# Two pairs of triangular inverses taken level by level together, and stores moved, in a two-layer decoder step

## Chip, cores and metric

The kernel runs on one NeuronCore of a Trainium2 chip (trn2). The metric is the device time of one execution in microseconds (us).

## What is computed

The program is one inference step of a two-layer hybrid decoder, for a prompt of 512 tokens and 8 samples of one token each (520 columns, model width 1024, all in f32). Both layers have a feed-forward block (SwiGLU, width 2816) before and behind a mixer. The first mixer joins gated linear attention with a gated DeltaNet; the second joins stick-breaking attention over paged keys and values with an RG-LRU. For this change three parts matter.

```
# gated DeltaNet, per head and chunk (the reference takes chunks of 64 rows; the kernel takes 128)
m     = eye + where(strict, (k k^T) * rel, 0) * beta     # unit lower triangular
w, u  = triangular_solve(m, [k * beta * exp(g), v * beta])
v_new = u - w @ s
o     = (q k^T * rel) @ v_new + (q * exp(g)) @ s
s     = s * exp(g_end) + (k * exp(g_end - g))^T @ v_new

# samples: the same with one token; each sample updates its own state
#   (8 x 4 states of 128x128 in DeltaNet, 8 x 4 of 64x128 in linear attention)

# stick-breaking, per head: z = q k^T * scale + bias
w = exp(log_sigmoid(z) + (sum over later keys of log_sigmoid(-z)));  o = w @ v

y_prompt, y_sample = rmsnorm(x)                           # the last outputs
```

## The kernel before, in words

Every engine has its own instruction list, written out by hand; semaphores join them. There is no scheduler: what stands where in a list decides. Most of the time goes into the projections (`unit`, `step`): weights come through SyncE's (SP) queue, ScalarE (ACT) and VectorE (DVE) split them into a high and a low part, and TensorE (PE) makes three products of each.

**The solve of the DeltaNet (`gdn` on each engine).** The prompt is four chunks of 128 tokens in two pairs (0: chunks 0 and 1, 1: chunks 2 and 3). Per chunk, `gdn_inputs(c)` makes the decays and the products k k^T and q k^T (PE: four groups of products; ACT: exponentials; DVE: `X`, `L21`), and on DVE `gdn_blocks(c)` cuts the lower triangle into the blocks of the levels (`cutB`). The inverse of a unit lower triangle is built in six levels, from blocks of 2 rows up to the two halves of 64. `gdn_first(p)` turns the first blocks of pair `p`. A level `l` of pair `p` is a chain over three engines:

- PE `level_products(p, l)`: `cutB` times `X` into PSUM (32 instructions),
- ACT `level(p, l)`: PSUM to `T1`,
- PE `level_merge(p, l, *steps)`: `X` times `T1`, both ways round (64 instructions),
- DVE `level(p, l)`: `X -= PSUM`; at level 5 it goes into the full inverse `DTf`, at level 6 only the lower left block is written.

Both pairs have banks of their own (pair 0: banks 4 to 7, pair 1: 0 to 3), so one can go on while the other waits. Into this chain other work is put:

- the 24 steps of the sample states: PE `update_rows(j)` spreads a row, ACT `update_products(j)` copies it scaled into `kvS` (four slots), DVE `update_states(j)` adds it to the state. They use one bank of the pair that is at rest (`state_bank`);
- the norms of linear attention: ACT `gla_squares`, PE `gla_sum`, ACT `gla_root`, DVE `gla_apply`, ACT `gla_high`, DVE `gla_low`, for four heads, and the same for the samples;
- products of ones and the identity that nothing reads (`idle_products`, and three at the head of `level_products(1, 4)` to `(1, 6)`), ahead of waits;
- behind a pair's last level `key_turns(c)`, DVE and ACT `key_copies(c)`, and `solve(c)`, which applies the inverse. Then come state and outputs, chunk by chunk, with the first output product in `gdn_outputs(0)`.

`LEVELS` lists the order of the twelve levels, `NTH` numbers them for the semaphores, and `STATES_BY` says how many sample steps must have left the banks. Before, pair 0 is up to five levels ahead of pair 1, and the inputs of chunks 2 and 3 stand between levels 1, 2 and 3 of pair 0.

**The samples' scores in stick-breaking (`mix_o` on GpSimd (POOL), `stick` on DVE).** In step `n` POOL waits for the scores of sample `n`, then sends the load of row `n + 2` of q (`load_q`, a broadcast to 128 partitions, `tmp<-q_rows`) and the two pages of `load_pages(n + 4)`. DVE `sample_scores(b)` multiplies them between its steps for the eight heads. The stores of the prompt's new values and keys (`out_sbv_p`, `out_sbk_p`, 1 MB each) are sent once, in one of these steps. The last four value pages go into `ktok` and wait for these stores.

**The end.** PE turns the eight tiles of the last norm back to rows, ACT copies each to `yrow` (semaphore `y_row`) and then the sample rows to `ysrow`; POOL stores `y_prompt` in two halves and `y_sample`.

## Time and profile before

| | |
|---|---|
| median of 3 runs | 2250.02 us (2247.71 to 2251.95) |
| the profiled execution, its own time | 2249.7 us |
| its span | 2248.1 us |
| mean granted clock of PE | 0.986 |
| PE busy | 2185.9 us, 97% of the span |
| DVE busy | 1068.2 us, 48% |
| ACT busy | 770.7 us, 34% |
| POOL busy | 67.7 us, 3% |

A timeline row merges like instructions that follow one another; in brackets stand the idle time of the engine before it and what ended it. A chain row is a piece of the path that ended last.

### The profile page before, as it was taken

To read this page: it belongs to the slowest core of one execution; us is meant where nothing else is said; L and a number is where in the kernel's file an instruction comes from. 1 tells how busy PE (TensorE), PEld (TensorE's weight loads), DVE (VectorE), ACT (ScalarE), POOL (GpSimd) and SP (SyncE) were. 2 spreads that over 40 slices of the span, in tenths; PEclk is the share of its full clock that TensorE was granted. 3 is DMA by queue.
4 is the path that set the end of the run, shared out by engine and by line. 5 is a ranking of instruction groups with operands and counts; after the bars stand their busy time and mean duration, and the time that the engine had idled before them with its cause. 6 is when DMAs were issued, how large, how long until landed. Compare 5 with 4: busy or idle time off the path is not lost.

```text
span 2248.1 us, 44698 instructions
## 1 busy us (share of the span) xinstructions
PE 2185.9 (97%) x18380; PEld 2124.4 (94%) x18380; DVE 1068.2 (48%) x1534; ACT 770.7 (34%) x1062; POOL 67.7 (3%) x143
## 2 busy tenths in 40 slices
PE   8999999999988999999999999999999899999996
PEld 7999999998877899999999999999996599999996
DVE  5444433586455554444334444433568444444332
ACT  5222222335244442222223222222357543222222
POOL 0000000100100000000000000000103200000000
PEclk9999999999988999999999999999999999999998
DMA  4333333432300332333233233323324323333331
GB/s 133 97 89 88 91 94 79 123 85 76 81 2 2 90 93 86 93 93 91 88 93 94 86 91 93 89 88 95 99 76 142 114 76 104 93 93 88 90 94 47
DMA packets 353651, 197.89 MB, mean 88 GB/s; under 512 B 10054, under 2 KB 348130, under 8 KB 353544
## 3 DMA queue, kind: packets, MB, share of 16 engines
q1 hardware_dynamic: 344640, 172.36, 26.6%
q0 software_dynamic: 6736, 21.97, 3.2%
q10 hardware_dynamic: 2176, 2.15, 0.3%
q8 instruction: 73, 1.20, 0.2%
q14 instruction: 26, 0.21, 0.0%
HBM read 188.52 MB, written 8.05 MB: 87 GB/s over the span
## 4 chain that ended last, share of the span: by engine, by line
PE 91%; DVE 4%; ACT 2%; issue 2%; DMA 1%; POOL 0%; DVEq 0%; ACTq 0%; POOLq 0%
PE PS L2174 81%; PE PS L2282 5%; PE PS L2849 1%; DVE wlo L1382 1%; PE PS L2768 0%; PE PS L2782 0%; DVE rawE L1419 0%; PE PS L2751 0%; PE PS L2834 0%; DVE tmp L1504 0%; PE PS L2654 0%; DMA tmp<-q_rows 0%; PE PS L2350 0%; PE PS L2189 0%; DMA prow_f<-in_ln_ffn 0%
## 5 line engine op out<-in xcount | busy, mean ns | idle before, releaser
L2174 PE MATMUL PS<-hh,whi 128*128 128x260 f32 x3600 | 730.9, 284 | 2.9 <-DVE hl L2099 1.7
L2174 PE MATMUL PS<-hh,wlo 128*128 128x260 f32 x3600 | 727.2, 284 | 0.0
L2174 PE MATMUL PS<-hl,whi 128*128 128x260 f32 x3600 | 726.3, 283 | 0.0
L1382 DVE TENSOR_TENSOR wlo<-stage,whi 128x1024 fp32r<-128x1024 f32 x337 | 412.3, 1223 | 449.5 <-ACT whi L778 439.7
L2174 PEld LDWEIGHTS PS<-hh,whi 128*128 128x128 f32 x3600 | 557.4, 189 | 5.8 <-DVE small L1521 1.5
L2174 PEld LDWEIGHTS PS<-hh,wlo 128*128 128x128 f32 x3600 | 556.6, 189 | 0.0
L2174 PEld LDWEIGHTS PS<-hl,whi 128*128 128x128 f32 x3600 | 555.2, 189 | 0.0
L778 ACT ACTIVATE whi<-stage 128x1024 fp32r<-128x1024 f32 x337 | 352.7, 1048 | 269.9 <-PE PS L2174 263.0
L2174 PE MATMUL PS<-act_h,whi 128*128 128x260 f32 x1408 | 284.3, 283 | 0.0
L2174 PE MATMUL PS<-act_h,wlo 128*128 128x260 f32 x1408 | 283.5, 283 | 0.0
L2174 PE MATMUL PS<-act_l,whi 128*128 128x260 f32 x1408 | 282.8, 282 | 0.0
L1419 DVE SCALAR_TENSOR_TENSOR tmp<-PS,rstd 128x520 f32<-128x520 f32 x176 | 123.0, 699 | 281.0 <-PE PS L2174 278.1
L2174 PEld LDWEIGHTS PS<-act_l,whi 128*128 128x128 f32 x1408 | 217.4, 188 | 0.0
L2174 PEld LDWEIGHTS PS<-act_h,whi 128*128 128x128 f32 x1408 | 217.0, 189 | 0.0
L2174 PEld LDWEIGHTS PS<-act_h,wlo 128*128 128x128 f32 x1408 | 216.9, 189 | 0.0
L823 ACT ACTIVATE act_h<-tmp 128x520 f32 (+1 forms) x88 | 56.2, 639 | 413.7 <-DVE tmp L1445 413.7
L820 ACT ACTIVATE tmp<-tmp 128x520 f32<-128x520 f32 x88 | 56.3, 639 | 286.8 <-DVE tmp L1419 286.8
L790 ACT ACTIVATE tmp<-xT 128x520 f32 (+1 forms) x48 | 30.7, 639 | 203.5 <-DVE xT L1459 203.5
L1448 DVE TENSOR_TENSOR act_l<-tmp,act_h 128x520 f32 (+1 forms) x88 | 61.7, 701 | 79.9 <-ACT act_h L823 79.9
L1459 DVE SCALAR_TENSOR_TENSOR xT<-PS,xT 128x520 f32 (+1 forms) x48 | 33.6, 700 | 96.1 <-PE PS L2174 96.1
L1445 DVE TENSOR_TENSOR tmp<-tmp 128x520 f32<-128x520 f32 x88 | 61.6, 700 | 3.0
L1398 DVE SCALAR_TENSOR_TENSOR hl<-xT,prm,hh x40 | 30.4, 760 | 64.2 <-ACT hh L792 64.2
(431 smaller groups left out, 1573.1 us busy)
## 6 DMA issues: line engine op xcount, KB each, us to landing
stage<-in_ffn_w_gate SPq DMA_DIRECT2D x88, 512.0 KB, 3.8
stage<-in_ffn_w_up SPq DMA_DIRECT2D x88, 512.0 KB, 3.8
stage<-in_ffn_w_down SPq DMA_DIRECT2D x64, 512.0 KB, 4.0
stage<-in_w_in_e SPq DMA_DIRECT2D x28, 512.0 KB, 3.8
stage<-in_ffn_w_down SPq DMA_DIRECT2D x32, 384.0 KB, 3.4
stage<-in_w_in_o SPq DMA_DIRECT2D x20, 512.0 KB, 3.7
stage<-in_w_out_e SPq DMA_DIRECT2D x8, 512.0 KB, 3.6
stage<-in_w_out_o SPq DMA_DIRECT2D x8, 512.0 KB, 3.6
```

Of the source, the lines that this page charges most:

```text
L778: act.activation(whi[:, s % SPLIT_SLOTS, :], stage[:, s % STAGE_SLOTS, :], ACT.Copy)\
L790: act.activation(tmp[:, slot, :], tile(xT, m), ACT.Square).then_inc(sq_ready, 1)
L820: act.activation(tmp[:, a, :], tmp[:, a, :], ACT.Silu).then_inc(gate_ready, 1)
L823: act.activation(act_h[:, bass.ds(2 * t + a, 1), :].rearrange("p a b -> p (a b)"), tmp[:, 2 + a, :], ACT.Copy).then_inc(act_hi, 1)
L1382: dve.tensor_tensor(wlo[:, slot, :], stage[:, s % STAGE_SLOTS, :], whi[:, slot, :].bitcast(F32), ALU.subtract).then_inc(lo_ready, 1)
L1398: dve.scalar_tensor_tensor(out=tile(hl, m), in0=tile(xT, m), scalar=prm[:, bass.ds(m + NORM_PRM[k], 1)], in1=tile(hh, m).bitcast(F32), op0 ...
L1419: return dve.scalar_tensor_tensor(out=dst, in0=psum, scalar=scale, in1=two(rstd[:]), op0=ALU.mult, op1=ALU.mult)
L1445: dve.tensor_tensor(tmp[:, 2 + a, :], tmp[:, a, :], tmp[:, 2 + a, :], ALU.mult)\
L1448: dve.tensor_tensor(tile(act_l, 2 * t + a), tmp[:, 2 + a, :], tile(act_h, 2 * t + a).bitcast(F32), ALU.subtract).then_inc(act_lo, 1)
L1459: dve.scalar_tensor_tensor(out=x, in0=psum, scalar=scale, in1=x, op0=ALU.mult, op1=ALU.add)\
L2174: mm = pe.matmul(psum[:, half, :], w, x(k)[:, half * HALF:(half + 1) * HALF], start=first and w is hi and x is rhs_hi, stop=last and w is lo)
L2282: return pe.matmul(out, w, x, start=True, stop=True)
```

## The change

It does three things.

- **Solve.** The inputs of chunks 2 and 3 and both `gdn_first` come ahead of all levels. Then both pairs take each level one behind the other, with four sample steps in each (two in each merge; at level 6 all four in pair 0's). The products without a reader are gone. The norms of linear attention go one to a level. Both solves, and the key turns before them, come after level 6 of both pairs.
- **Stick-breaking.** The two 1 MB stores are sent in step 6 of the sample loop instead of step 4.
- **End.** SP stores `y_prompt` in four quarters as they are ready, and `y_sample`; DVE copies the sample rows.

```diff
-        LEVELS = [(0, 1), (0, 2), (0, 3), (0, 4), (1, 1), (0, 5), (1, 2), (0, 6), (1, 3), (1, 4), (1, 5), (1, 6)]
+        LEVELS = [(p, l) for l in range(1, 7) for p in range(2)]
-        STATES_BY = {(p, l): 3 * (l - 1) if p == 0 else 21 if l == 6 else 0 for p, l in LEVELS}
+        STATES_BY = {(p, l): 4 * (l - 1) if p == 0 else 0 for p, l in LEVELS}
-            return banks((4 if j < 18 else 0) + j % 2, 1)
+            return banks(4 + j % 2, 1)
...
+            for a in range(4):
+                sp.wait_ge(y_row, KD // 4 * (a + 1))
+                part = slice(a * DM // 4, (a + 1) * DM // 4)
+                sp.dma_start(o["y_prompt"][0].rearrange("(b p) n -> p b n", p=P)[:, :, part], yrow[:, :, part])\
+                  .then_inc(stored, 16)
+            sp.wait_ge(ys_row, 2)
+            sp.dma_start(o["y_sample"][:, 0, :], ysrow[:]).then_inc(stored, 16)
+            sp.wait_ge(stored, 80)
...
-                    if n == TS // 2:
+                    if n == TS - 2:
                         pool.wait_ge(v_rows, 1 + NB)
                         save(o["sbv_p"][0, 0].rearrange("(c p) h d -> p c (h d)", p=P), vtok[:])
...
```

ACT's list in `gdn`, now:

```diff
+                gdn_inputs(2)
+                gdn_inputs(3)
+                gla_squares(0)
                 gdn_first(0)
+                gdn_first(1)
+                gla_root(0)
+                for l in range(1, 7):
+                    level(0, l)
+                    if l < 4:
+                        gla_squares(l)
+                    level(1, l)
+                    states(*range(4 * l - 4, 4 * l))
+                    if l < 4:
+                        gla_root(l)
+                    if l == 3:
+                        samples_squares()
+                    elif l == 4:
+                        samples_root()
+                    elif l == 5:
+                        samples_high()
+                    if 1 <= l <= 4:
+                        gla_high(l - 1)
                 key_copies(0)
                 solved(0)
                 key_copies(1)
                 solved(1)
```

DVE's:

```diff
                 gdn_inputs(2)
                 gdn_inputs(3, 2)
                 gdn_blocks(3)
+                for l in range(1, 7):
+                    states(4 * l - 4, 4 * l - 3)
+                    if l == 6:
+                        states(22, 23)
+                    level(0, l)
+                    if l == 6:
+                        key_copies(0)
+                    else:
+                        states(4 * l - 2, 4 * l - 1)
+                    if l < 5:
+                        gla_apply(l - 1)
+                    elif l == 5:
+                        samples_apply()
+                    if 2 <= l <= 5:
+                        gla_low(l - 2)
+                    level(1, l)
+                samples_low()
                 key_copies(1)
                 next_state(0)
```

PE's:

```diff
             def level_merge(p, l, *steps):
-                if (p, l) in ((0, 1), (0, 2), (1, 4), (1, 5), (1, 6)):
-                    idle_products(p, 2)
-                elif (p, l) == (0, 3):
-                    idle_products(p, 1)
                 pe.wait_ge(gb_t1c, 2 * (NTH[p, l] + 1))
+                for j in steps:
+                    update_rows(j)
                 if p == 1 and l < 4:
                     gla_sum(l)
...
+                gdn_inputs(2)
+                gdn_inputs(3)
                 gdn_first(0)
                 gdn_first(1)
                 gla_sum(0)
+                for l in range(1, 6):
+                    level_products(0, l)
+                    level_products(1, l)
+                    level_merge(0, l, 4 * l - 4, 4 * l - 3)
+                    level_merge(1, l, 4 * l - 2, 4 * l - 1)
+                level_products(0, 6)
+                level_products(1, 6)
+                level_merge(0, 6, 20, 21, 22, 23)
                 key_turns(0)
+                level_merge(1, 6)
                 solve(0)
                 key_turns(1)
                 solve(1)
                 state_products(0)
                 gdn_outputs(0)
```

What this does to the lists themselves shows at two places. In them `X,cutB` are level products, `small,ident` and `prE` the products of a chunk's inputs, `ident,X` a pair's first turn and `tmp,ones` a norm sum. First PE's list from the end of the sample read (the turn of `vnS`) through level 1 of pair 0, before:

```order
L2849 MATMUL PS<-ident,vnS 32x128 [waits sa_vn]
L2282 MATMUL PS<-ident,X 64x64 [waits sa_o,sa_rc,gb_dt0]
L2282 MATMUL PS<-ident,X 64x64 x15
L2282 MATMUL PS<-X,cutB 64x64 [waits gb_d0c]
L2282 MATMUL PS<-X,cutB 64x64 x15
L2282 MATMUL PS<-small,ident 128x128 [waits gb_eg]
L2282 MATMUL PS<-small,ident 128x128 x3
L2282 MATMUL PS<-prE 128x128 [waits gb_out]
...
L2282 MATMUL PS<-ident,ones 128x128 x2
L2282 MATMUL PS<-vaR,ident 64x256 [waits gb_t1c]
```

The same stretch up to the first level, now:

```order
L2787 MATMUL PS<-ident,vnS 32x128 [waits sa_vn]
L2247 MATMUL PS<-small,ident 128x128 [waits gb_eg]
L2247 MATMUL PS<-small,ident 128x128 x3
L2247 MATMUL PS<-prE 128x128 [waits gb_out]
...
L2247 MATMUL PS<-ident,X 64x64 [waits sa_o,sa_rc,gb_dt0]
L2247 MATMUL PS<-ident,X 64x64 x15
L2247 MATMUL PS<-ident,X 64x64 [waits gb_eg,gb_out,gb_dt0]
L2247 MATMUL PS<-ident,X 64x64 x15
L2247 MATMUL PS<-tmp,ones 128x260 [waits hn_sq]
L2247 MATMUL PS<-tmp,ones 128x260
L2247 MATMUL PS<-X,cutB 64x64 [waits gb_d0c]
L2247 MATMUL PS<-X,cutB 64x64 x15
```

The inputs' products (for both chunks) and the turns of both pairs now stand ahead of the first level product; before, the turn of pair 0 and its level 1 came first.

Second, POOL's list in step 4 and 5 of the sample loop, before:

```order
L696 DMA out_sbv_p<-vtok 128x4x512 [waits v_rows]
L696 DMA out_sbk_p<-ktok 128x4x512 [waits k_rows]
L729 AFFINE_SELECT own<-own 128x8
L729 AFFINE_SELECT own<-own 128x8 [waits consts]
L680 DMA tmp<-q_rows 128x512 [waits sm_kq,consts]
L687 TENSOR_LOAD ptab
```

and in the steps 5 and 6, now:

```order
L683 DMA tmp<-q_rows 128x512 [waits sm_kq,consts]
L690 TENSOR_LOAD ptab
...
L694 DMA pages<-in_cache_sb_v 128x512
L699 DMA out_sbv_p<-vtok 128x4x512 [waits v_rows]
L699 DMA out_sbk_p<-ktok 128x4x512 [waits k_rows]
L690 TENSOR_LOAD ptab
L694 ISA
L694 DMA prO<-in_cache_sb_v 128x512
```

The load of the last q row (`tmp<-q_rows`) stood behind the two stores and now stands ahead of them.

## Rows read from the trace of the kernel before

**Rows 1.** Busy time by stretch: length, PE, PEld, DVE, ACT, POOL, PE clock, DMA.
```profile
641.00:740.00 99.00, 86.98 (x1363) 77.22 (x1364) 52.23 (x120) 40.99 (x124) 2.38 (x6) 0.86 0.01 2
704.00:714.00 10.00, 9.77 (x81) 8.33 (x82) 4.65 (x12) 4.46 (x13) 0.00 (x0) 0.52 0.01 2
```
**Rows 2.** The chain of waits in the solve: start us, us, what.
```profile
640.85 0.19 DVE prE L1900
...
739.88 1.09 PE PS L2567 x8
740.97 0.89 PE PS L2849 x8
...
743.23 3.80 PE PS L2282 x26
```
**Rows 3.** Timeline, inputs and blocks of chunk 3, then pair 1's first turn.
```profile
660.44 0.69 DVE L1670 SCALAR_TENSOR_TENSOR prE<-relB,PS 128x512 f32<-128x512 f32 x1 [1.40 <-ACT relB L985]
...
663.85 0.15 DVE L1685 TENSOR_TENSOR colS<-colS,colGB 128x4 f32<-128x4 f32 x1
...
667.60 1.49 DVE L1693 TENSOR_TENSOR cutB<-X,blocks 128x1280 f32<-128x1280 f32 x1
...
669.94 1.79 PE L2282 MATMUL PS<-ident,X 64*64 64x64 f32 x32 [0.96 <-DVE X L1697]
```
**Rows 4.** Timelines of PE, DVE and ACT in the levels.
```profile
692.94 1.15 PE L2282 MATMUL PS<-X,cutB 64*64 64x64 f32 x32 [0.58 <-DVE X L1707]
694.02 1.15 PE L2282 MATMUL PS<-vnR,ident 32*128 32x128 f32 x8
...
696.07 0.68 PE L2282 MATMUL PS<-T,X 64*64 64x64 f32 x16
...
698.08 1.15 PE L2282 MATMUL PS<-tmp,ones 128*128 128x260 f32 x4
...
704.23 1.93 PE L2282 MATMUL PS<-X,cutB 64*64 64x64 f32 x32 [2.23 <-DVE X L1707]
...
698.23 0.42 DVE L1710 TENSOR_TENSOR X<-X,PS 128x256 f32<-128x256 f32 x1 [1.04 <-PE PS L2282]
...
700.66 0.76 DVE L1756 SCALAR_TENSOR_TENSOR prE<-prE,prm,tmp 128x520 f32<-128x520 f32 x1
...
702.80 1.28 DVE L1707 TENSOR_TENSOR X<-X,PS 128x512 f32<-128x512 f32 x2
...
694.76 1.14 ACT L1195 ACTIVATE kvS<-PS,prE 128x128 f32<-128x128 f32 x4
```
**Rows 5.** Timelines of DVE, POOL and PE in stick-breaking.
```profile
1751.41 1.23 DVE L2048 TENSOR_TENSOR tmp<-pages,tmp 128x1024 f32<-128x1024 f32 x1 [2.90 <-DMA tmp<-q_rows]
...
1744.40 0.56 POOL L680 DMA_DIRECT2D tmp<-q_rows  x1 [0.30 <-POOL own L729]
...
1745.26 1.02 PE L2768 MATMUL PS<-skX,upto 128*128 128x512 f32 x2
...
1748.84 2.37 PE L2782 MATMUL PS<-skZ,vtok 128*64 128x512 f32 x8
...
1758.27 2.05 PE L2768 MATMUL PS<-skX,upto 128*128 128x512 f32 x2 [4.08 <-DVE skR L2005]
...
1763.98 2.37 PE L2782 MATMUL PS<-skZ,vtok 128*64 128x512 f32 x8
...
1777.46 1.10 PE L2768 MATMUL PS<-skX,upto 128*128 128x512 f32 x2 [1.63 <-DVE skR L2005]
```
**Rows 6.** The end: timeline, then DMA issues with KB each and us to landing.
```profile
2233.72 2.78 ACT L1365 ACTIVATE yrow<-PS 128x512 f32<-128x512 f32 x5 [0.40 <-PE PS L2849]
...
2238.02 0.53 POOL L575 DMA_DIRECT2D out_y_sample<-ysrow  x1
...
out_y_sample<-ysrow POOLq DMA_DIRECT2D x1, 32.0 KB, 5.2
...
stage<-in_ffn_w_up SPq DMA_DIRECT2D x88, 512.0 KB, 3.8
```

More of the change, by code:

```diff
@@ L411, in build_step @@
             sem(n) for n in "gate_read gate_ready up_read prod_ready act_hi act_lo".split())
-        y_row, stored = sem("y_row"), sem("stored")
+        y_row, ys_row, stored = sem("y_row"), sem("ys_row"), sem("stored")
         y_t, SETUP_T = setup_t, 4 + KD
@@ L563, in _ @@
                     tiles4(FIRST["out_o0"], tiled(i["w_out_o"][0]), 0, 0, KD // 4)
+            for a in range(4):
[6 more added lines that the diff above has]
+            sp.wait_ge(stored, 80)
         @block.gpsimd
         def _(pool):
-            stores = 0
-            def store(dst, src):
-                nonlocal stores
-                stores += 1
-                pool.dma_start(dst, src).then_inc(stored, 16)
             pool.memset(ones[:], 1.0).then_inc(consts, 1)
@@ L753, in _ @@
                     mix_o()
-            for a in range(2):
-                pool.wait_ge(y_row, KD // 2 * (a + 1))
-                part = slice(a * DM // 2, (a + 1) * DM // 2)
-                store(o["y_prompt"][0].rearrange("(b p) n -> p b n", p=P)[:, :, part], yrow[:, :, part])
-            pool.wait_ge(y_row, KD + 2)
-            store(o["y_sample"][:, 0, :], ysrow[:])
-            pool.wait_ge(stored, 16 * stores)
             if ("mix_e", 0) in STAGES:
@@ L1366, in _ @@
                    .then_inc(y_row, 1)
-            for a in range(2):
-                act.activation(ysrow[:, a * 512:(a + 1) * 512], banks(4 + a, 1)[0:TS, :], ACT.Copy).then_inc(y_row, 1)
         @block.vector
@@ L1800, in gdn @@
                 gdn_inputs(2)
-                states(0, 1, 2)
-                level(0, 1)
                 gdn_inputs(3, 2)
-                states(3, 4, 5)
-                level(0, 2)
                 gdn_blocks(3)
-                states(6, 7, 8)
-                level(0, 3)
-                states(9, 10, 11)
-                level(0, 4)
-                gla_apply(0)
-                level(1, 1)
-                states(12, 13, 14)
-                level(0, 5)
-                gla_apply(1)
-                gla_low(0)
-                level(1, 2)
-                states(15, 16, 17)
-                level(0, 6)
-                gla_apply(2)
-                gla_low(1)
-                level(1, 3)
-                key_copies(0)
-                gla_apply(3)
-                gla_low(2)
-                level(1, 4)
-                gla_low(3)
+                for l in range(1, 7):
[15 more added lines that the diff above has]
+                samples_low()
                 key_copies(1)
-                samples_apply()
-                states(18, 19, 20)
-                level(1, 5)
-                samples_low()
                 next_state(0)
-                states(21, 22, 23)
-                level(1, 6)
                 key_copies(2)
@@ L2151, in _ @@
             last_norm()
+            dve.wait_ge(y_t, SETUP_T + KD)
+            for a in range(2):
+                dve.tensor_copy(ysrow[:, a * 512:(a + 1) * 512], banks(4 + a, 1)[0:TS, :]).then_inc(ys_row, 1)
         @block.tensor
@@ L2418, in level_products @@
                 if l > 1:
-                    if p == 1 and l in (4, 5, 6):
-                        for _ in range(3):
-                            mm1(level_bank(p, 1, 0)[:, 0:P], ones[:], ident[:])
                     pe.wait_ge(gb_ddc, 2 * (NTH[p, l - 1] + 1))
@@ L2454, in chunk_sum @@
                 mm1(banks(6 + c % 2, 1), ones[:], sqC).then_inc(hn_sum, 1)
-            def idle_products(p, n):
-                for _ in range(n):
-                    mm1(level_bank(p, 0, 1)[:, 0:P], ones[:], ident[:])
             def level_merge(p, l, *steps):
-                if (p, l) in ((0, 1), (0, 2), (1, 4), (1, 5), (1, 6)):
-                    idle_products(p, 2)
-                elif (p, l) == (0, 3):
-                    idle_products(p, 1)
                 pe.wait_ge(gb_t1c, 2 * (NTH[p, l] + 1))
+                for j in steps:
+                    update_rows(j)
                 if p == 1 and l < 4:
@@ L2471, in level_merge @@
                     samples_sum()
-                for j in steps:
-                    update_rows(j)
                 if l == 6:
@@ L2497, in key_turns @@
                     pe.wait_ge(gb_ddc, 2 * (NTH[0, 6] + 1))
-                    pe.wait_ge(sa_kv, 36)
+                    pe.wait_ge(sa_kv, 2 * STEPS)
                 elif c == 2:
```

61 lines of the change are left out of this document (removed).

## Prediction

> **What bounds the kernel now.** I read the views from coarse to fine: busy shares and granted clock by stretch, then the chain of waits, then the timelines of the three places that the diff touches. Outside these places nothing can change: TensorE (PE) is 97% busy over the span (the table above), with the weight products of the projections. Three places are not bound by it.
>
> The first is the delta-rule solve. The stretch from 641 to 740 us has PE busy for 87.0 of 99 us at a mean granted clock of 0.86 [rows 1]. A clock is either whole (2.4 GHz) or half (1.2 GHz), so 0.86 means that 28% of it, some 27 us, ran at half; at the whole clock the same products need about 74 us. The chain of waits goes through this stretch from the end of the sample read (640.85) to the first output product (739.88): 99.0 us [rows 2]. That distance is the term to forecast.
>
> The second is stick-breaking attention. VectorE (DVE) stands 2.90 us before the score product of the last sample, and the wait ends with the row of q that it needs (`tmp<-q_rows`); GpSimd (POOL) issued that load at 1744.40, behind two stores of 1 MB. PE stood 4.08 us for DVE and then ran the sums of a head from 1758.27 to 1763.98, 5.71 us; the head before took 3.58 us for the same (1745.26 to 1748.84) [rows 5]. The first product took 2.05 us instead of 1.02, the half clock again.
>
> The third is the end. The last copy of y ends at 2236.50; POOL issues the last halves after it and the last one lands 5.2 us after 2238.02, at 2243.2 [rows 6]. The 4.9 us from there to the end of the span are the program's close and stay.
>
> **The solve, step by step.** Before, the two chunk pairs were staggered, and inputs of chunks 2 and 3 were made between levels of the first pair. Now all inputs come first and both pairs take each level together.
>
> *Entry.* PE can start the inputs of chunk 2 at once (its waits are long met), so the first exponentials come about 1.7 us after 640.85 (an estimate from eight products and four ScalarE (ACT) copies). Then DVE has everything: inputs of a chunk take 3.6 us (660.44 to 664.0) and its blocks 2.3 us (667.60 to the first product that waited for them, 669.94) [rows 3]. Twice both is 11.8 us, so pair 1's blocks are ready 13.5 us in. PE, done with its part after some 8 us, stands about 5 us. That gap surely costs the clock: gaps of 2.2 us did, the next products being 1.93 us instead of 1.15 [rows 4]. So pair 1's first turn takes 1.8 us [rows 3] and the sum for the norm 2.1 (twice 1.08). Entry: 1.7 + 11.8 + 1.8 + 2.1 = 17.4 us.
>
> *Levels 1 to 5.* At the whole clock the products of a pair take 1.08 us (692.94 to 694.02), three sample-state products 2.05 (694.02 to 696.07, two in some 1.0), a merge 2.0 (696.07 to 698.08), the norm sum 1.08 [rows 4]. A level in step is 2 x 1.08 + 4 updates 2.0 + 2 merges 4.0 + norm sum 1.08 = 9.2 us of PE. To it comes a wait: pair 1's next products need DVE's subtraction (1.28 us [rows 4]), of which the products of pair 0 cover 1.08; with two handovers 0.45 us remain. DVE has between pair 0's subtraction and pair 1's: the subtraction 1.28, two steps of states about 1.1 (as long as ACT's copies for them, 1.14 us), and the norm's apply and low part 2.14 (700.66 to 702.80) = 4.6 us, against PE's 1.0 + 1.08 + 2.0 = 4.1. So from level 3 on DVE is 0.5 us late; at level 4, where the norm sum is small, 1.3 us, which level 5 pays. Levels: 10.2 (the first at half clock in part, no wait), 9.7, 10.2, 9.4, 9.9 = 49.4 us.
>
> The filler products that go (40 instructions) stood directly ahead of waits, so they free PE but shorten the chain by little; I count nothing for them beyond the levels above.
>
> *Level 6 and the two solves.* Little is left to interleave here. Pair 1's subtraction of level 5 starts 1.7 us late and takes 2.4 us (698.23 to 700.66 [rows 4]); its products, its copy and the copies of four sample steps (1.14 us for two [rows 4]) follow: 7.3 us until the last sample product, 8.8 until pair 0's block is written, 9.8 after the key turns. Key turns to solve are 2.3 us (740.97 to 743.23 [rows 2]), a solve some 2 us, and both come twice, now one after the other: 18.6 us in all to the output products. Before, pair 0's solve lay under pair 1's levels.
>
> Sum at these speeds 17.4 + 49.4 + 18.6 = 85.4 us. **The clock** is the open term. In level 6 PE stands 3 us and then works about half of the time. I take 4 us for a loss there (dips before cost up to 5: from 704 to 714 us the mean clock was 0.52 [rows 1]) and 1.4 for one dip somewhere in the levels: 90.8 us, **8.2 us less** than 99.0. Ends: no dips in tail or levels gives 13.6 less; dips as long as before's 27 us, half of it lost, give 85.4 - 2.8 (already counted in the entry) + 13.6 = 96.2, still 2.8 less. What follows 739.88 is the same work.
>
> **The page stores.** Sent two samples later (after the loads that the last sample needs), they no longer stand before the q row: POOL issues it near 1741.9, it lands in some 4 us and DVE wants it at 1748.5. So 2.9 us go. DVE's next steps then make PE stand 1.3 us, and after a gap of 1.63 us the first product still took 1.10 [rows 5], so the half clock goes as well: 5.71 - 3.58 = 2.1 us. Together **5.0 less**, taken as 4.9; the low end is 2.5. Late next: the last four value pages wait for these stores to land. They were loaded by 1766 and will be at about the same time, while their products begin near 1785, so this cover is 15 us or more. I count zero.
>
> **The final stores.** SyncE (SP), idle since the last weights, sends four quarters of 512 KB as ACT completes them; DVE copies the sample rows while ACT still works. The last quarter goes at 2236.6. Weight loads of that size through SP land in 3.8 us [rows 6], so 2240.4, and the small sample store with it: **2.8 less**. Ends: 5.2 us as on POOL's queue gives 1.4; 2.5 us gives 4.1. The Trainium skill ("DMA: Bandwidth & Descriptors", specifications) gives first bytes after about 1 us from GpSimd and 0.6 us from the sync path; by it alone the store would save 0.4 us rather than 2.8. The rows say that most comes from smaller last pieces and from not waiting for the sample copy.
>
> **Sum.** The profiled execution took 2249.7 us, 0.3 below the median: 2249.7 - 8.2 - 4.9 - 2.8 = 2233.8, with the 0.3 about 2234 us.
>
> **The rivals.**
> 1. *The lockstep keeps PE at the half clock* (slower). Level products fill only a 64 x 64 part of the array and sample products have few rows, the fillers (full 128 x 128) are gone, and each level has a gap. For it: from 704 to 714 us the clock stayed at half though PE was busy for 9.8 of the 10 us [rows 1]. Against it: from 692.94 to 700 the same kinds of products ran whole, behind a gap of 0.58 us and with no filler among them [rows 4]. Price: a level at half is 2 x 9.2 us less the hidden wait, 8 us more. The gains of 15.9 us are used up when two levels run wholly at half; with three, 2234 + 24 = 2258 us. The Trainium skill ("TensorE: Matmul & The Clock Gate", the section on a second failure mode) says that frequent short idles between groups of products alone can make the clock go up and down; by it this rival would be the rule in each level and the removed fillers a loss. The trace before half agrees: mean 0.86 even with them.
> 2. *The stagger was worth as much* (small gain). If waits of DVE and ACT, which I took as hidden, add 1.5 us to each level, the solve gains nothing and only the stores do: 2234 + 8 = 2242 us.
> 3. *No clock loss outside the entry*: 2234 - 5.4 = 2229 us.
> 4. *The moved stores delay the value pages* past their products: they would have to slip by over 15 us for 1 us; hardly possible.
>
> **How the numbers follow.** Forecast 0.55 (2230 to 2238), rival 2 with its neighbours 0.22 (to 2244), rival 3 0.12, rival 1 0.1 (half of it above 2250), rival 4 0.01. A range of 2228 to 2244 leaves out rival 1 and the ends of rival 3, some 15 to 20 in 100. A measurement of this kernel can tell 0.2% or 4.5 us from no change. Faster by more is the forecast, rival 3 and nearly all of rival 2: 0.89; within it the rest of rival 2 and a part of rival 1: 0.06; slower 0.05.
>
> **What would show it.** Right: the chain from the sample read to the first output product near 91 us, PE standing about 5 us once before the first level, levels of 9.5 to 10.5 us, a mean clock near 0.9; no wait of DVE on `tmp<-q_rows`, and sums of every head near 3.6 us; last landing 4 us after the last copy of y. Wrong: levels beyond 12 us or a clock under 0.8 in them (rival 1), DVE busy without a break from 641 to 700 with PE standing over 2 us in each level (rival 2), or output stores on SP that take over 5 us to land.

## The result and the profile after

The changed kernel takes 2232.06 us in the median of 4 runs (2228.76 to 2235.55), the kernel before 2250.78 us beside it: a ratio of 0.9919, interval 0.9897 to 0.9942, so 18.7 us less by the medians. The forecast was 2234.0 us, in a range of 2228 to 2244. A second comparison (the changed kernel once more, in the second group of runs below) gave 2235.44 us and 0.9942, interval 0.993 to 0.9955, so 13 us less. Both together say 13 to 19 us.

The profiled execution took 2228.76 us, span 2227.1 us; before it was 2249.7 us, span 2248.1 us. Laid side by side, the two spans differ by 21.0 us:

| stretch | before | after | forecast |
|---|---|---|---|
| start of the program to the end of the sample read | 640.9 | 638.4 | same |
| sample read to the first output product (the solve) | 99.0 | 91.6 | 90.8 |
| to the transfer of the q rows, `q_rows<-rowS` (projections, feed-forward) | 965.0 | 964.9 | same |
| stick-breaking, to the last sample products | 88.2 | 84.8 | -4.9 |
| to the first copy of y | 437.5 | 437.5 | same |
| first copy of y to the end of the span | 17.5 | 9.9 | -2.8 |

The first line is not the change: the code there is the same, and one stretch at half clock was shorter in this execution. The other three that moved are the three places of the prediction.

A stretch of one execution is not yet the stretch of the kernel. With the solve untouched, the profiled executions of two later runs (the end alone, the page stores alone) took 94.8 us for it, not 99.0. The kernel before ran at half clock from 643 to 650 us in its profiled execution, and these two did not. First the kernel before, then the one with the end alone (length, PE, PEld, DVE, ACT, POOL, PE clock, DMA):

```profile
643.00:650.00 7.00, 6.89 (x56) 6.77 (x57) 0.69 (x1) 2.60 (x11) 0.34 (x1) 0.52 0.01 4
```
```profile
643.00:650.00 7.00, 6.71 (x78) 5.53 (x76) 3.81 (x10) 3.83 (x15) 0.63 (x1) 1.00 0.01 4
```

So up to 4 of the 7.4 us between the two rows of the solve belong to that execution. The old end, too, took 16.4 to 16.5 us in three other runs, not 17.5. What each part is worth is taken from the runs of the parts below.

**The solve.** Busy time by stretch of the changed kernel (length, PE, PEld, DVE, ACT, POOL, PE clock, DMA), the whole solve and then its pieces:

```profile
638.42:730.03 91.61, 77.50 (x1318) 69.51 (x1317) 51.49 (x120) 40.55 (x124) 2.38 (x6) 0.87 0.01 2
645.98:650.70 4.72, 0.00 (x0) 0.00 (x0) 4.55 (x10) 1.18 (x3) 0.63 (x1) 0.96 0.00 0
650.70:657.10 6.40, 6.00 (x74) 5.02 (x76) 0.35 (x1) 1.91 (x5) 0.00 (x0) 0.50 0.00 0
657.10:708.14 51.04, 44.27 (x1039) 38.94 (x1035) 34.00 (x82) 25.81 (x79) 1.11 (x4) 1.00 0.01 3
708.14:725.60 17.46, 16.62 (x96) 15.30 (x96) 5.34 (x15) 5.48 (x16) 0.00 (x0) 0.51 0.01 1
```

Read it from the clock column. PE stands idle while DVE makes chunk 3's blocks (5.12 us up to pair 1's first turn), then runs at half clock until 657.1, which takes in the first products of level 1. From there the five levels run at the whole clock. Level 6 and the solves run at half for 17.5 us, with PE busy for 16.6 of them. Against [rows 1], half clock now lies in two pieces, the entry and the end, instead of spread over the stagger, and its share is the same (0.87 against 0.86). Timeline rows of PE, pair 1's first turn and its first products of level 6, behind the two long waits:

```profile
651.10 1.97 PE L2247 MATMUL PS<-ident,X 64*64 64x64 f32 x32 [5.12 <-DVE X L1674]
...
708.14 1.73 PE L2247 MATMUL PS<-X,tmp 64*64 64x64 f32 x16 [3.36 <-DVE cutB L1691]
```

The chain of waits has one level between two of these starts of PE (start us, us, what):

```profile
666.71 4.22 PE PS L2247 x104
...
676.65 4.30 PE PS L2247 x104
680.97 1.29 DVE X L1684 x2
682.26 1.05 DVE stB_s L1875 x4
683.31 0.68 DVE prE L1733
684.01 0.70 DVE prE L1734
684.71 0.61 DVE oE L1743
685.32 1.20 DVE X L1684 x2
686.66 4.30 PE PS L2247 x104
...
696.68 4.30 PE PS L2247 x104
...
730.03 0.97 PE PS L2520 x8
```

666.71, 676.65, 686.66, 696.68: a level is 9.9 to 10.0 us. More than half of it is DVE: its two subtractions (L1684), and between them the sample states and the apply and low pieces of the norm (L1733 to L1743).

**Stick-breaking.** Timelines of DVE and PE (start us, us, engine, line, operation, count, idle before it and what ended that):

```profile
1737.19 1.29 DVE L1973 TENSOR_TENSOR oO<-prO,oO 128x520 fp32r<-128x520 f32 x2
1738.40 1.22 DVE L2011 TENSOR_TENSOR tmp<-pages,tmp 128x1024 f32<-128x1024 f32 x1
...
1745.29 1.31 PE L2706 MATMUL PS<-skX,upto 128*128 128x512 f32 x2 [1.08 <-DVE skR L1968]
...
1750.61 2.37 PE L2720 MATMUL PS<-skZ,vtok 128*64 128x512 f32 x8
```

The score product of the last sample follows on its predecessor: the wait of 2.90 us on the q row [rows 5] is gone. PE waits 1.08 us for DVE instead of 4.08, but the first products still take 1.31 us, and the head's sums take 5.32 us (1745.29 to 1750.61) instead of the 3.6 expected. Half clock stayed in this execution.

**The end.** Timeline of ACT, DVE and SP's queue, then busy time of the last 2.6 us:

```profile
2218.91 4.81 SPq L568 DMA_DIRECT2D out_y_prompt<-yrow  x4
...
2220.43 2.90 ACT L1344 ACTIVATE yrow<-PS 128x512 f32<-128x512 f32 x5 [0.47 <-PE PS L2787]
...
2222.72 1.28 DVE L2117 COPY ysrow<-PS 8x512 f32<-8x512 f32 x2 [1.54 <-PE PS L2787]
2224.03 0.32 SPq L571 DMA_DIRECT2D out_y_sample<-ysrow  x1
```
```profile
2224.50:2225.50 1.00, 0.00 (x0) 0.00 (x0) 0.00 (x0) 0.00 (x0) 0.00 (x0) 1.00 1.08 383
2225.50:2226.50 1.00, 0.00 (x0) 0.00 (x0) 0.00 (x0) 0.00 (x0) 0.00 (x0) 1.00 0.76 262
2226.40:2227.10 0.70, 0.00 (x0) 0.00 (x0) 0.00 (x0) 0.00 (x0) 0.00 (x0) 1.00 0.00 0
```

From the end of the last copy of y to the end of the span are 3.8 us (2223.33 to 2227.1); before it was 11.6 (2236.50 to 2248.1, [rows 6]). The last two columns show data moving in the second row and none in the third: the last data move before 2226.4, and the program is over 0.7 us later. The kernel before, read in the same way, has 5.3 us there (2242.8 to 2248.1). The 4.9 us after the last landing, which the prediction let stand, are not there.

### The profile page after: what moved, and what is told of

Read it like the earlier page. It is cut to its first block, busy times and chain, and to the rows that moved or that the text cites. A ratio compares the mean times of both kernels' runs of the same rounds, so it can differ in the third digit from the quotient of the medians.

```text
span 2227.1 us, 44620 instructions
## 1 busy us (share of the span) xinstructions
PE 2173.3 (98%) x18340; PEld 2114.3 (95%) x18340; DVE 1068.7 (48%) x1536; ACT 769.6 (35%) x1060; POOL 66.5 (3%) x140
## 4 chain that ended last, share of the span: by engine, by line
PE 90%; DVE 6%; ACT 2%; issue 1%; DMA 0%; DVEq 0%; ACTq 0%
PE PS L2139 81%; PE PS L2247 4%; PE PS L2787 1%; DVE wlo L1359 1%; PE PS L2706 1%; PE PS L2720 0%; PE PS L2689 0%; DVE X L1684 0%; DVE rawE L1396 0%; PE PS L2709 0%; DVE tmp L1481 0%; PE PS L2772 0%; PE PS L2592 0%; PE PS L2154 0%; PE PS L2315 0%
```

## The experiments

Twelve runs were made, in three groups; each group has its own runs of the kernel before. Times are medians, and what a part brings is taken from its ratio. Executions of the kernel before range over 8 us within one group (2245.12 to 2252.65 in the second), so beside each ratio I read the lengths of the stretches in the profiled execution (us; the solve here from PE's timeline, up to 0.2 shorter than by the chain):

| profiled execution | solve | stick-breaking | last feed-forward | end |
|---|---|---|---|---|
| before | 99.0 | 88.2 | 437.5 | 17.5 |
| the end alone | 94.8 | 88.6 | 437.5 | 11.3 |
| the page stores alone | 94.8 | 83.2 | 439.0 | 16.5 |
| the solve alone | 89.2 | 87.8 | 437.5 | 16.4 |
| only the fillers out | 92.2 | 87.6 | 437.5 | 16.5 |
| changed | 91.5 | 84.8 | 437.5 | 9.9 |
| changed once more | 90.4 | 84.7 | 440.0 | 9.8 |
| quarters on POOL | 93.1 | 83.2 | 437.5 | 16.2 |
| products in the gaps | 88.2 | 84.8 | 437.5 | 9.9 |
| sample work later | 88.3 | 84.8 | 437.5 | 9.8 |
| both edits | 85.2 | 84.8 | 437.5 | 9.9 |
| both, without 10 products | 86.2 | 83.1 | 437.5 | 11.7 |
| both, stores on POOL | 85.3 | 84.8 | 437.5 | 15.8 |
| both, more products | 84.3 | 83.2 | 439.0 | 9.9 |

One and the same code differs by up to 4 us in the solve and by 1.7 us in stick-breaking from one row to another. A difference within that is not put down to an edit by the stretch alone.

### Each part of the change alone

**The end alone**: the kernel before with these hunks of the change only.

```diff
-            for a in range(2):
-                pool.wait_ge(y_row, KD // 2 * (a + 1))
...
+            for a in range(4):
+                sp.wait_ge(y_row, KD // 4 * (a + 1))
...
+            dve.wait_ge(y_t, SETUP_T + KD)
+            for a in range(2):
+                dve.tensor_copy(ysrow[:, a * 512:(a + 1) * 512], banks(4 + a, 1)[0:TS, :]).then_inc(ys_row, 1)
```

> The kernel before with the change's end alone (four quarters of y_prompt and y_sample from SP, sample rows copied by DVE). Theory A (the 4.9 us between the last landing and the end of the span belonged to POOL's stores): the distance from the last square of the last norm (24.8 us before, 17.1 us with the whole change) falls to about 17.1 us, and the median by 7.6 us. Rival, the prediction's own term (the close is fixed and only pieces and the copy count): 22 us and 2.8 us less.

2241.29 us, ratio 0.9974 (0.9965 to 0.9983), so 5.8 us less, 3.8 to 7.9 by the interval; first copy of y to the end of the span 11.3 us instead of 17.5, which is 6.2 less, or 5.2 against the 16.5 of the other runs with the old end. My 2.8 us lie outside all of these. The term was half of what the part brings.

**The page stores alone**: `if n == TS - 2:` in place of `if n == TS // 2:`.

> The kernel before with the two 1 MB stores sent in step 6 instead of 4, nothing else. Theory: DVE's wait of 2.9 us on the q row goes, and the stretch from the first load of q to the first output projection falls from 90.2 us by 2.9 to 5.0 us: 2.9 where PE drops to half clock all the same in the sums of head 5 (as with the whole change, 86.8 us), 5.0 where it does not. Rival (the stores collide with the value pages): no gain, and PE waits at the value products.

2243.77 us, ratio 0.9985 (0.9976 to 0.9994), 3.4 us less. The stage took 83.2 us instead of 88.2, and PE's first product after the wait 1.10 us:

```profile
1750.48 1.10 PE L2768 MATMUL PS<-skX,upto 128*128 128x512 f32 x2 [1.08 <-DVE skR L2005]
```

The wait is the same 1.08 us as in the changed kernel, where half clock followed and the products took 1.31. So the wait alone does not decide it. Nor does the kernel's own code in this stage: the changed kernel's stage took 84.8 us in most of the profiled executions and 83.2 and 83.1 in two (quarters on POOL, both without 10 products), whose stage code is the same.

**The solve alone**: the table of levels, the order of ACT, DVE and PE, no fillers.

> The kernel before with the new order of the solve alone. Theory: the distance from the end of the sample read to the first output product falls from 99.0 to about 91.6 us as with the whole change, and the median by 7 to 8 us; with the two others 7.4 + 3.4 + 7.6 = 18.4 us, the whole measured difference (18.7). Rival (the parts are not independent, for one the start of the program or the phase of the clock makes a part of it): a difference of under 4 or over 11 us.

2240.01 us, ratio 0.9971 (0.9962 to 0.9979), 6.5 us less, 4.7 to 8.5 by the interval. The stretch was 89.2 us where 91.6 was expected: 9.8 less than in the kernel before's execution, 5.6 less than the 94.8 of the two runs with the old solve and the fillers. The three singles sum to 15.7 us, within the 13 to 19 of the whole: they act in different places, and nothing speaks against their adding up.

**Only the fillers out**, from the kernel before.

```diff
-                    if p == 1 and l in (4, 5, 6):
-                        for _ in range(3):
-                            mm1(level_bank(p, 1, 0)[:, 0:P], ones[:], ident[:])
...
-                if (p, l) in ((0, 1), (0, 2), (1, 4), (1, 5), (1, 6)):
-                    idle_products(p, 2)
-                elif (p, l) == (0, 3):
-                    idle_products(p, 1)
```

> The kernel before without the products that nothing reads (20 in the solve). Theory (they stand ahead of waits and hardly lengthen the chain): within 1.5 us of before, with a mean clock from 641 to 740 us of 0.80 to 0.90. Rival 1 of the prediction (they are what keeps the clock up): the mean clock falls below 0.80 and the stretch grows by 3 us or more.

2248.13 us, ratio 1.0002 (0.999 to 1.0015). In the median, taking out the 20 filler products (40 instructions) costs and brings nothing, as the prediction had counted. The ten executions fall into two groups, though: three took 2238.79 to 2241.12 us, less than any of the 35 of the kernel before (2243.59 the lowest), and seven 2246.95 to 2251.72. The profile is of the fastest one; its solve took 92.2 us at a mean clock of 0.93, above the 0.80 to 0.90 expected. The fillers do not hold the clock up there; what made the two groups no run shows.

### Where the end's gain comes from, and what the solve still loses

**The changed kernel once more**, as the base of the second group.

> The changed kernel itself once more, as the base of this call: ratio to before 0.992 (0.990 to 0.994), some 17 to 19 us. Theory A (the three parts add up, 5.8 + 3.4 + 6.5 = 15.7 us by the single-part runs): 0.993. Rival B (together they give more than apart, 18.7 us as first measured): 0.9917.

2235.44 us, ratio 0.9942 (0.993 to 0.9955): 13.0 us less, against 15.7 for the sum of the singles, so they do not give more together than apart. In its profiled execution the last feed-forward, whose code is untouched, took 440.0 us from stick-breaking to the first copy of y, instead of 437.5. This is the spread between executions, and it is half clock: PE ran at half around 1786 us too, and longer than in the first profile in the last norm, from 2214 us on.

**Quarters on POOL**: the changed kernel with the five final stores issued by POOL, `pool.` for `sp.` in the first diff above and nothing else.

> The changed kernel, but the five final stores are issued by POOL again (in quarters, after each quarter's ACT copies, as now on SP). Theory A: what came back at the end beyond the shorter chain of copies and issue is the time between the last landing and the end of the program, which exists only with final stores on POOL (4.9 us before, none after): from the last yrow copy's end to the span's end 3.8 us becomes some 8, and the kernel is 4 to 5 us slower than the changed one. Rival B (the engine that issues them does not matter, the finer pieces and the earlier start do): within 1 us of the changed kernel.

2236.39 us, ratio 0.9951 (0.9939 to 0.9964). By the medians only 1 us slower, as rival B had it; but the end stretch is 16.2 us long instead of 9.8, as theory A had it. The two readings disagree. In the profiled executions the base lost 2.5 us in the last feed-forward and 1.5 in stick-breaking that this kernel did not lose, and this one lost 2.7 in the solve; none of this code differs. I repeated this test later on a base with less spread.

This execution showed one thing more. Its solve took 93.0 us, and a stretch of the fifth level ran at half clock (busy time by stretch, columns as above):

```profile
700.00:708.00 8.00, 8.00 (x101) 7.36 (x98) 3.63 (x11) 3.07 (x10) 0.00 (x0) 0.54 0.01 2
```

PE's wait before it is 1.41 us, the same as in the changed kernel's profile, which kept the clock. So the levels are not safe from half clock; they escaped it in the other nine profiled executions with the new order.

**Products in the gaps**: 20 products that nobody reads in the entry gap, 12 ahead of pair 1's level 6.

```diff
                 gdn_first(0)
+                for _ in range(20):
+                    mm1(banks(4, 1)[:, 0:P], ones[:], ident[:])
                 gdn_first(1)
...
                 level_products(0, 6)
+                for _ in range(12):
+                    mm1(level_bank(1, 0, 0)[:, 0:P], ones[:], ident[:])
                 level_products(1, 6)
```

> The changed kernel with 20 reader-less products of 128x128 by PE between the two pairs' first products (where PE waits 5.1 us for X and then runs at half clock until 657) and 12 ahead of pair 1's level-6 products (where it waits 3.4 us and then runs at half clock until 725.6). Theory A (the idle stretch is what takes the clock, and half the idle time filled is enough): the solve's 91.4 us becomes 85 to 88, 3 to 6 us faster than the changed kernel. Rival B (as the run without fillers, where the kernel's time did not move): within 1 us of the changed kernel. Rival C (the added products delay the waiting ones, or a later stretch pays for it): slower by 1 to 3 us.

2227.61 us, ratio 0.9909 (0.9896 to 0.9921). The solve is 88.2 us; with the changed kernel's order it took 89.2, 90.4, 91.5 and 93.1. The entry keeps its clock. Timeline of PE:

```profile
648.00 4.73 PE L2247 MATMUL PS<-ident,ones 128*128 128x128 f32 x40
653.21 1.15 PE L2247 MATMUL PS<-ident,X 64*64 64x64 f32 x32 [0.47 <-DVE X L1674]
...
708.09 1.11 PE L2247 MATMUL PS<-X,tmp 64*64 64x64 f32 x16 [0.49 <-DVE cutB L1691]
709.13 1.15 PE L2247 MATMUL PS<-vnR,ident 32*128 32x128 f32 x8
710.60 2.04 PE L2247 MATMUL PS<-vnR,ident 32*128 32x128 f32 x8 [0.31 <-ACT kvS L1174]
```

At the entry pair 1's first turn takes 1.15 us, the whole clock's time, where the changed kernel's took 1.97. Pair 1's products of level 2 begin 26.2 us into the solve instead of 28.0 in the base, so the filled entry gives 1.8 us. At level 6 the wait shrinks from 3.36 to 0.49 us, and yet the same eight products take 1.15 us at 709.13 and 2.04 us at 710.60: half clock sets in within a stretch that is nearly full. The executions also lie close together (2226.7 to 2227.69). Of the 7.8 us to the base's median, 2.2 are in the solve of the two profiles and 2.5 in the last feed-forward, which no edit touched; the others are not located. The changed kernel's first four executions lie in two groups, 2228.76 and 2229.11, 2235.0 and 2235.55, and its repeat had none under 2232.86. So a part of the 7.8 us may be the base's spread; whether the products act on later stretches too, no run tests.

**The sample work later on DVE**: `gla_low` behind `level(1, l)` instead of ahead of it.

> The changed kernel with the sample work on DVE (the low pieces, 0.69 us per level) behind pair 1's level copies instead of ahead of them. Theory A (DVE's own chain per level, 10.0 us, is the bound, and what stands in it ahead of pair 1's copies delays PE): each level's wait of PE before pair 1's products (0.6 to 1.4 us) shrinks, 0.3 to 0.6 us per level, 2 to 3 us in all. Rival B (DVE is busy all the time whatever the order, so the same work only moves to before pair 0's next copies): within 1 us.

2228.88 us, ratio 0.9914 (0.9902 to 0.9927), the solve 88.3 us. PE's waits in the levels, total, times and longest, in the changed kernel and then here:

```profile
PE PS L2247 <- DVE X L1684: 3.4, 4, 1.4
```
```profile
PE PS L2247 <- DVE X L1684: 2.5, 4, 0.8
```

and the level starts of PE here are 9.8, 9.9 and 9.4 us apart (670.01, 679.79, 689.71, 699.12), where the changed kernel had 9.9, 10.0 and 10.0. The last two, then level 6:

```profile
689.71 1.15 PE L2247 MATMUL PS<-X,cutB 64*64 64x64 f32 x32 [0.58 <-DVE X L1684]
...
699.12 1.15 PE L2247 MATMUL PS<-X,cutB 64*64 64x64 f32 x32 [0.80 <-DVE X L1684]
...
709.97 1.11 PE L2247 MATMUL PS<-X,tmp 64*64 64x64 f32 x16 [2.75 <-DVE cutB L1691]
```

What stood ahead of pair 1's copies on DVE was on the path, in the way theory A says, but unevenly: the waits shrink by 0, 0.17, 0.09 and 0.61 us, and the one before level 6 from 3.36 to 2.75, together 1.5 us. In the levels these waits are the same to 0.01 us in every profiled execution of either order. The rest of the shorter solve is where the clock fell, about 1.5 us into level 6 instead of at its first products. By the medians this kernel is 6.6 us faster than the base, which the waits do not explain; the spread of the base's executions, as above, may be in it.

### Both together, and the end again

**Both edits** (with 10 products at level 6, whose wait is shorter in this order).

> The changed kernel with both edits that were faster alone: the sample work on DVE behind pair 1's copies, and the added products (20 in the entry gap, 10 ahead of pair 1's level-6 products, where the other order leaves 2.75 us). Theory A (they act on different waits and add): solve 88.3 us less the entry's 3 us and 0 to 1 at level 6, so 84 to 86, the kernel 2223 to 2226, ratio 0.9895 to 0.990. Rival B (both remove the same half-clock stretches): 2227 to 2229, as each alone.

2224.89 us, ratio 0.9891 (0.9876 to 0.9906), the solve 85.2 us. They add: the solve is 3.0 us shorter than with the products alone and 3.1 us shorter than with the order alone.

**The same without the 10 products at level 6.**

> As the run with both edits, but without the 10 products at level 6. Theory A: with 12 products there the engine was busy but for 0.5 us from 704.7 on and the clock still fell at 710.7, so these products give nothing but what their own 0 to 1 us are: within 1 us of the run with both edits. Rival B: without them the tail loses 1.5 to 3 us more.

2224.29 us, ratio 0.9898 (0.9883 to 0.9913). No difference in time; the solve's stretch was 86.2 us, 1 us longer. What the 10 products buy is at most about that. Against the order alone (88.3 us) this kernel has the 20 products at the entry and nothing else, 2.1 us less.

**Both edits, final stores on POOL.**

> As the run with both edits, with the five final stores issued by POOL (in quarters). It differs from that run in the last 17 us alone, and that base had little spread between executions. Theory A (a final store issued by POOL ends the program later: in the profile of the changed kernel with such stores the last sample store's issue ended 8.4 us before the span's end, against 2.8 us with SP): 5 to 6.5 us slower than the run with both edits, about what the end alone gave. Rival B (the median of the changed kernel moved by 1 us only, so the profile's close is not in the time that counts): 0.5 to 2 us slower.

2231.18 us (2228.63 to 2234.88) against 2224.89 (2222.58 to 2225.2): 6.3 us slower, and no execution of the one overlaps one of the other. With SP first, the timeline of ACT and SP's queue at the end, then busy time while the last data move and behind them:

```profile
2216.33 2.78 ACT L1344 ACTIVATE yrow<-PS 128x512 f32<-128x512 f32 x5 [0.36 <-PE PS L2791]
...
2219.82 0.32 SPq L571 DMA_DIRECT2D out_y_sample<-ysrow  x1
```
```profile
2221.00:2222.00 1.00, 0.00 (x0) 0.00 (x0) 0.00 (x0) 0.00 (x0) 0.00 (x0) 1.00 1.16 409
2222.40:2223.10 0.70, 0.00 (x0) 0.00 (x0) 0.00 (x0) 0.00 (x0) 0.00 (x0) 0.84 0.00 0
```

The same two views of the kernel with its final stores on POOL:

```profile
2216.10 2.78 ACT L1344 ACTIVATE yrow<-PS 128x512 f32<-128x512 f32 x5 [0.36 <-PE PS L2791]
...
2219.92 0.54 POOL L755 DMA_DIRECT2D out_y_sample<-ysrow  x1
```
```profile
2222.00:2223.00 1.00, 0.00 (x0) 0.00 (x0) 0.00 (x0) 0.00 (x0) 0.00 (x0) 0.83 0.96 356
2223.50:2228.80 5.30, 0.00 (x0) 0.00 (x0) 0.00 (x0) 0.00 (x0) 0.00 (x0) 0.50 0.00 0
```

The copies run alike, and the last store is issued 3.5 us (SP) and 3.8 us (POOL) after the start of this row of copies. In steps of 0.1 us the last data move before 2222.4 with SP, and the span ends at 2223.1. With POOL they move until 2223.5 and the span ends at 2228.8.

So there are 5.3 us in which nothing is busy and nothing moves, against 0.7. Read in the same way, all profiled executions agree: 5.1 to 5.3 us in the six with the final stores on POOL (5.3 in the kernel before), 0.6 to 0.8 in the eight with them on SP. Which engine has these stores decides whether that time exists. The edit moves the issue of the stores and the wait for their landing together, so the runs do not tell which of the two it is. They also show what the finer pieces and DVE's copy are worth: with both and the stores on POOL the end took 16.2 and 15.8 us, with neither 16.4 to 16.5 (17.5 in the kernel before), so under 1 us.

**More products**: 5 in the 0.84 us wait before the key turns, 6 ahead of head 5's sums in stick-breaking.

> As the run with both edits, with 5 more products in PE's 0.84 us wait before the first key turns (for DVE's copy of pair 0's level-6 blocks) and 6 in the 1.08 us wait of the stick stage ahead of head 5's sums, where half clock follows until 1750.6. Theory A (a short wait is what takes the clock there): the stick stage 84.8 becomes 83.2 (the 1.7 us of one half-clock stretch), the solve's tail gets whole clock from 716 on, 4 us; together 2 to 6 us faster. Rival B (the tail's half clock has another cause, since it set in while PE was busy): the stick's 1.7 us alone. Rival C (the added products delay the next work by their own time at half clock, 1.4 us in the tail): no gain in the tail or 1 us lost.

2222.49 us (2221.39 to 2223.76), ratio 0.9882 (0.9867 to 0.9897), the fastest version that ran. Stick-breaking took 83.2 us instead of 84.8, the 1.6 us of theory A; but two kernels without these products took 83.1 and 83.2 as well, so this is not shown to be their work. The solve took 84.3 instead of 85.2, and the half clock of its tail was shorter, not gone. Busy time by stretch, with both edits alone and then with the added products:

```profile
657.00:704.00 47.00, 44.43 (x1039) 39.17 (x1039) 31.05 (x75) 24.84 (x76) 1.11 (x4) 1.00 0.01 3
703.90:707.00 3.10, 2.78 (x26) 2.57 (x25) 2.95 (x9) 0.88 (x3) 0.00 (x0) 1.00 0.00 0
707.00:710.00 3.00, 2.69 (x30) 2.44 (x28) 1.36 (x5) 1.79 (x6) 0.00 (x0) 1.00 0.01 3
710.00:722.00 12.00, 10.86 (x68) 9.87 (x67) 4.41 (x13) 3.48 (x10) 0.00 (x0) 0.57 0.00 1
```
```profile
710.00:718.00 8.00, 8.00 (x55) 7.48 (x55) 3.60 (x10) 1.88 (x7) 0.00 (x0) 0.57 0.01 2
718.00:726.00 8.00, 6.62 (x59) 6.38 (x58) 2.40 (x5) 3.82 (x9) 0.00 (x0) 1.00 0.00 0
```

The clock came back at about 717 us instead of 721 (the same 721 in the kernel with stores on POOL). So the wait before the key turns seems to prolong the half clock (one execution with the wait filled, two without); it does not start it. PE was busy for 2.8 of 3.1 and 2.7 of 3.0 us when the clock fell at 710, and for 44.4 of 47 us of the levels when it did not. Why it falls there stays open; all four kernels with products ahead of level 6 show it, between 710 and 711. Without such products a wait of 1.9 to 3.4 us stands directly ahead of pair 1's level 6, and the clock falls in it or within 2 us behind it. Whether this run gains anything over both edits is not settled either: the intervals overlap, and of its 2.4 us only the 0.9 in the solve lie in a stretch that no kernel without the added products matched.

## Why the prediction was right, step by step

The total was right to 2 us against the first measurement and to 1.4 against the second. That is in part luck: two terms were too large (page stores, and by the single part the solve too) and one too small by about as much (final stores).

*The solve, 8.2 us less.* Measured 7.4 by the chain of waits of the two profiled executions, 6.5 by the single part. The 99.0 us that the term starts from held a half-clock stretch (643 to 650 us) which two other executions of the same solve did not have; against their 94.8 the changed solve is 2 to 6 us shorter. Entry: PE stood 5.12 us (5 forecast), half clock followed, and the first level's products began at 655.03, 16.6 us in, where I had 17.4. Levels 1 to 5: 49.8 us against 49.4 (9.9, 10.0, 10.0 us from start to start of levels 2 to 5, where I had 9.7, 10.2, 9.4 for levels 2 to 4). DVE's lateness came much as forecast: the waits were 0.58, 0.75 and 0.67 us, and 1.41 behind level 4, whose norm sum is small. The run with the sample work later showed a part of it, 0.9 us in all, to be DVE's order. "1.4 for one dip somewhere in the levels" was not there: the clock was 1.00 over 51 us. "I take 4 us for a loss" in the tail was too little: 17.5 us at 0.51, and from PE's wait before level 6 (704.8) to the output products 25.2 us instead of 22.6. Half of PE's 16.6 busy us is a loss of 8, so the work itself was nearer 17 us than my 18.6 (whose own parts add up to 18.4). Together with the shorter entry these leave 0.8 us.

*Page stores, 4.9 us less.* Measured 3.4 in the profile of the change, 3.4 by the single part (1.3 to 5.4). "These 2.9 us go" held. The step that failed is "the half clock goes as well: 2.1 us", which I read off one row after a gap of 1.63 us. The page-stores run bore it out (1.10 us for the products), the changed kernel did not (1.31), after the same wait. What a short wait costs differs from one execution to the next with the same code around it (84.8 or 83.2 us for the stage); one row with a whole clock behind a gap is a chance, not a rule. The size to take was 2.9, with 2.1 more as the other end.

*Final stores, 2.8 us less.* Measured 7.6 in the profile, 5.8 by the single part. The failed step is "The 4.9 us from there to the end of the span are the program's close and stay". The landing was right within a microsecond: data out 3.1 us after the last copy, 3.9 forecast. But I took the idle time after it for a fixed cost, though it was on record in one kernel only, and in that one POOL held the last stores. The run on POOL with all else equal brought it back, 5.3 us without data where SP had 0.7, and 6.3 us of time. "Most comes from smaller last pieces and from not waiting for the sample copy" failed as well: these gave under 1 us. The Trainium skill ("DMA: Bandwidth & Descriptors", specifications) has 0.4 us between the two ways, for the first byte; no run here shows that apart. The difference of the whole end is some fifteen times as large.

*The rivals.* Rival 1 (half clock in the levels) fell as the rule: PE had a wait in each of four levels and kept 1.00, and of ten profiled executions with the new order only the one with quarters on POOL lost a level to it (10 us at half clock). The section on a second failure mode in the Trainium skill's "TensorE: Matmul & The Clock Gate" would have had the clock go up and down there; the traces disagree for the levels but for that one, and the fillers, whose loss it would count against the change, were worth nothing in the median (1.0002). Its mechanism does show in one place, level 6 and the tail, for 8 us and not 24. Rival 2 (stagger worth as much) fell with the solve's own 6.5 us, although its sign, DVE pacing the levels, was partly there: waits of 0.6 to 1.4 us in each level. Rival 3 (no loss outside the entry) fell with the tail. Rival 4 fell too: PE did not wait for the last four value pages, and the stretch to the last sample products only became shorter.

## What to carry to other kernels

- Do not take idle time after the last landing for a fixed cost: see which engine issues the last stores and waits for them, and let SP do it where it is idle. Here this was worth 6 us, the finer pieces and the earlier copies under 1.
- Where two chains go in step and the vector engine hands over between them, its order inside a step is on the path: put what nobody waits for behind the second chain's copies (1.5 us of PE's waits here for one moved line). Filling the one large gap of PE (5 us) gave 1.8 to 2.1 us; that filling small ones (0.6 to 1.4 us) gives anything is not shown.
- With an edit worth less than the spread of executions, read the length of its own stretch in the profile beside the medians, and repeat it on a base that spreads little; the medians alone gave 1 us for an effect of 6. But read that stretch in several executions: one profile of the kernel before had 4 us in the solve that others of the same code had not.

## What the runs showed of the hardware that was not expected

- With final stores on POOL, 5.1 to 5.3 us pass from the last data to the end of the span (six executions, the kernel before among them); with them on SP 0.6 to 0.8 us (eight executions).
- The cost of a PE wait varies. The same 1.08 us wait in stick-breaking was followed by half clock in the changed kernel and not in the one with the page stores alone; an untouched stretch of 437.5 us took 440.0 in another execution, and the untouched solve 94.8 us in two and 99.0 in one. The Trainium skill ("TensorE: Matmul & The Clock Gate", "What's actually happening") says of the slow products at a kernel's start that their number varies from run to run. That these stretches vary too agrees with it in kind; the start itself is not what they show.
- The clock fell with PE busy for 2.7 of the last 3 us at the start of the solve's tail in the kernel with both edits, and near the same place in the three others with products ahead of level 6; it did not in the levels just before (44.4 of 47 us busy). Nothing here explains it.
